# A mixture-of-experts stage on one Trainium2 core: wide and narrow experts of a pair run one after the other, or by turns in slices of 512 gate columns

## The reference, cut to what matters

```
h = rms_norm(x); top 2 of 8 experts by h @ w_router; weights by softmax over the two
for each expert e, for its tokens:
    out += weight * ((silu(h @ w_gate[e]) * (h @ w_up[e])) @ w_down[e])   # 1024 -> 3584 -> 1024
```

## Time and profile before

| what | us |
|---|---|
| median of 3 runs | 1788.53 |
| the profiled execution, and its span | 1787.69, 1785.9 |
| first expert matmul starts | 883.07 |
| first wide expert ends, its narrow one starts | 1002.16 |
| second pair starts | 1107.26 |
| last expert matmul starts | 1776.20 |

### The profile page before, as it was taken

How to read it: one execution, slowest core, us unless ns; L and a number is a source line. 1 busy time by engine, 2 the same in 40 slices (tenths; PEclk the granted TensorE clock), 3 DMA queues, 4 the chain that set the end, 5 groups by cost and what they waited for, 6 DMA issues and landing times.

```text
span 1785.9 us, 22528 instructions
## 1 busy us (share of the span) xinstructions
PE 1677.6 (94%) x8602; PEld 1246.9 (70%) x8602; DVE 1104.5 (62%) x1395; ACT 931.7 (52%) x1162; POOL 21.3 (1%) x30
## 2 busy tenths in 40 slices
PE   9988999999999999999899978999789997899987
PEld 7877788888878888987688524885248852488622
DVE  7985799757668874676898303883029840298400
ACT  6976677556755553664577203773027730277300
POOL 0000000000000000000000000000000000000000
PEclk9999999999999999999999999999999999999988
DMA  9332355544225554334399999999999999999997
GB/s 376 143 112 95 142 189 189 189 171 147 108 95 194 189 197 175 142 142 142 118 370 368 355 422 415 417 372 347 422 415 417 373 344 421 419 418 382 340 422 302
DMA packets 68941, 490.94 MB, mean 275 GB/s; under 512 B 7776, under 2 KB 8160, under 8 KB 9952
## 3 DMA queue, kind: packets, MB, share of 16 engines
q1 hardware_dynamic: 67248, 484.48, 69.5%
q0 software_dynamic: 1584, 4.98, 1.4%
HBM read 485.24 MB, written 4.19 MB: 274 GB/s over the span
## 4 chain that ended last, share of the span: by engine, by line
PE 76%; DMA 12%; DVE 6%; ACT 4%; issue 2%; POOL 0%; SPq 0%; DVEq 0%; ACTq 0%; POOLq 0%
PE ps L460 14%; PE ps L469 13%; PE ps L462 13%; DMA raw<-in_units 12%; PE ps L596 9%; PE ps L1345 8%; PE ps L599 5%; PE ps L480 1%; DVE wl L2360 1%; PE ps L900 1%; PE ps L901 1%; PE ps L905 1%; PE ps L1364 1%; PE ps L1317 1%; PE ps L471 1%
## 5 line engine op out<-in xcount | busy, mean ns | idle before, releaser
L3394 DVE TENSOR_TENSOR wl<-raw,wh 128x2048 fp32r<-128x2048 f32 x160 | 365.6, 2291 | 40.2 <-ACT wh L2238 39.9
L2238 ACT ACTIVATE wh<-raw 128x2048 fp32r<-128x2048 f32 x156 | 299.1, 1917 | 90.0 <-PE ps L469 90.0
L2360 DVE TENSOR_TENSOR wl<-raw,wh 128x2048 fp32r<-128x2048 f32 x124 | 283.0, 2286 | 81.8 <-ACT wh L1564 81.5
L460 PE MATMUL ps<-wh,hT_both 128*128 128x512 f32 (+2 forms) x680 | 268.9, 397 | 15.2 <-ACT wh L2224 8.2
L1564 ACT ACTIVATE wh<-raw 128x2048 fp32r<-128x2048 f32 x125 | 238.4, 1913 | 70.2 <-PE ps L469 69.0
L1345 PE MATMUL ps<-raw,hT_f 128*64 128x512 f32 x448 | 218.7, 637 | 58.5 <-DMA raw<-in_units 58.4
L462 PE MATMUL ps<-wh,hT_both 128*128 128x512 f32 (+2 forms) x680 | 262.5, 388 | 0.0
L3375 DVE TENSOR_TENSOR work<-work,ps 128x256 f32<-128x256 f32 x28 | 11.8, 421 | 370.2 <-ACT work L2212 370.2
L1346 PE MATMUL ps<-raw,hT_f 128*64 128x512 f32 x448 | 219.5, 639 | 0.0
L1345 PEld LDWEIGHTS ps<-raw,hT_f 128*64 128x64 f32 x448 | 61.2, 145 | 188.2 <-issue 188.2
L469 PE MATMUL ps<-wl,hT_both 128*128 128x512 f32 (+2 forms) x680 | 181.9, 385 | 0.2 <-DVE wl L3394 0.2
(11 more groups left out here) (480 smaller groups left out, 2343.8 us busy)
## 6 DMA issues: line engine op xcount, KB each, us to landing
raw<-in_units SPq DMA_DIRECT2D x458, 1024.0 KB, 7.8
x<-in_x SPq DMA_DIRECT2D x2, 512.0 KB, 5.5
work<-in_lru_w SPq DMA_DIRECT2D x1, 1024.0 KB, 15.8
xn<-in_mem SPq DMA_DIRECT2D x1, 1024.0 KB, 15.0
out<-x POOLq DMA_DIRECT2D x2, 512.0 KB, 6.8
consts<-in_consts POOLq DMA_DIRECT2D x1, 768.0 KB, 4.7
consts<-in_consts SPq DMA_DIRECT2D x1, 500.0 KB, 11.8
cols<-in_cols SPq DMA_DIRECT2D x1, 202.0 KB, 2.3
```

Source lines behind the costliest of these rows:

```text
L460: nc.tensor.matmul(out, sh, mh, start=(first and j == 0), stop=False)
L2238: A(wh[:, n % SPLIT, :], raw[:, n % RAW, :], ACT.Copy).then_inc(sem("hi_made"), 1)
L2360: V.tensor_tensor(wl[:, n % SPLIT, :], raw[:, n % RAW, :], wh[:, n % SPLIT, :].bitcast(F32), ALU.subtract).then_inc(sem("lo_made"), 1)
L3394: V.tensor_tensor(wl[:, n % SPLIT, :], raw[:, n % RAW, :], wh[:, n % SPLIT, :].bitcast(F32), ALU.subtract).then_inc(sem("lo_made"), 1)
```

## The change

The two experts of a pair are no longer run one after the other. For each chunk `c` (a slice of 512 gate columns) every engine does the wide expert's part and then the narrow expert's part: TensorE runs wide gate c, up c and down c-1, then narrow gate and up c and down c-1, then the wide chunk's transposes. The order of loads is a table, `STREAM`: per slice 6 wide units (three of them already of the next slice, since splitting runs 3 units ahead) and then 6 narrow ones. At a pair's end the next pair's first three wide units are loaded ahead of the narrow expert's last two. The number of units, matmuls and splits stays the same. The PSUM banks and the small buffers are laid out anew, so that both experts live side by side; both tiny row and weight gathers of a pair move to slice 3, and ScalarE reads both at once. Both address tables are read up front: the queue now waits for `ordered` before it loads the eighth unit of the stage, where before it loaded the whole first wide expert without it.

```diff
+STREAM = [(0, 0, _u) for _u in EXPERT_ORDER[:SPLIT]]
+for _p in range(NPAIR):
+    for _c in range(ECH):
+        _at = 6 * _c + (1 if _c == 0 else -2) + (2 if _c == 0 else 3)
+        _wide = EXPERT_ORDER[_at:_at + (4 if _c == 0 else 6)]
+        STREAM += [(_p, 0, _u) for _u in _wide] + [(_p, 1, _u) for _u in NARROW_ORDER if _u[1] == _c - (_u[0] == "down")]
+    STREAM += [(_p + 1, 0, _u) for _u in EXPERT_ORDER[:SPLIT] if _p + 1 < NPAIR]
+    STREAM += [(_p, 1, ("down", ECH - 1, _h)) for _h in range(2)]
...
@@ TensorE
+            for c in range(ECH):
+                if c > 0:
+                    pe.wait_ge(sem("gate_silu"), ECH * p + c)
+                wide_in("gate", c)
+                if c > 0:
+                    narrow_turned(c - 1)
+                    pe.wait_ge(sem("hidden"), ECH * p + c + 2)
+                wide_in("up", c)
+                if c > 0:
+                    pe.wait_ge(sem("expert_hid"), ECH * p + c)
+                    if c == 1:
+                        pe.wait_ge(sem("y_scaled"), 4 * p + 2)
+                    for half in range(2):
+                        wide_down(c - 1, half)
+                if c == 3:
+                    pe.wait_ge(sem("weighted"), 2 * p + 2)
+                    for i, (places_by, rows_by) in enumerate(((Gw, row_and_gate), (narrow_weights, narrow_rows))):
+                        for t in range(TT):
+                            ins = nc.tensor.matmul(ps[:, 2, 4 * i:4 * i + 4], places_by[:, t, :], rows_by[:, t, :],
+                                                   start=(t == 0), stop=(t == TT - 1))
+                    ins.then_inc(sem("bank7_full"), 2)
...
+                narrow_in(c, 0)
+                if c == ECH - 1:
+                    wide_turned(c)
+                narrow_in(c, 1)
+                if c == ECH - 1:
+                    pe.wait_ge(sem("expert_hid"), ECH * (p + 1))
+                    for half in range(2):
+                        wide_down(c, half)
+                if c > 0:
+                    for half in range(2):
+                        narrow_down(c - 1, half)
+                if c < ECH - 1:
+                    wide_turned(c)
+            narrow_turned(ECH - 1)
+            if not last:
+                pe.wait_ge(sem("chosen"), p + 2)
+                for q in range(4):
+                    gather(q, LATER_BANKS)
+            for half in range(2):
+                narrow_down(ECH - 1, half)
...
@@ SyncE
         def freed(n):
-            s, j = (n - N_FIXED) // E_UNITS, (n - N_FIXED) % E_UNITS
-            if s % 2 == 0:
-                sp_.wait_ge(sem("lo_made"), N_FIXED + s // 2 * E_UNITS + j + 1)
+            p, narrow, what = STREAM[n - N_FIXED]
+            if narrow:
+                sp_.wait_ge(*reached("narrow_gu", p * E_UNITS + NARROW_OF[what] + 1))
             else:
-                sp_.wait_ge(*reached("narrow_gu", s // 2 * E_UNITS + j + 1))
+                sp_.wait_ge(sem("lo_made"), N_FIXED + p * E_UNITS + UNIT_OF[what] + 1)
         sp_.wait_ge(sem("ordered"), 1)
-        for s in range(1, NE):
-            at = nc.sync.value_load(order[0:1, s:s + 1], min_val=N_FIXED, max_val=N_FIXED + (NE - 1) * E_UNITS)
...
+        at = [nc.sync.value_load(order[0:1, s:s + 1], min_val=N_FIXED, max_val=N_FIXED + (NE - 1) * E_UNITS) for s in range(NE)]
+        for n in range(N_FIXED + RAW, N_UNITS):
+            p, narrow, what = STREAM[n - N_FIXED]
+            freed(n - RAW)
+            load(None, n, units_d[at[2 * p + narrow] + UNIT_OF[what]])
@@ ScalarE
+            for c in range(ECH):
+                hi(UNIT_OF["up", c, 1])
+                if c > 0:
+                    hi(UNIT_OF["down", c - 1, 0])
+                    narrow_silu(c - 1)
+                wide_silu(c)
+                if c > 0:
+                    hi(UNIT_OF["down", c - 1, 1])
+                if c == 3:
+                    act.wait_ge(sem("bank7_full"), 6 * p + 6)
+                    act.wait_ge(sem("out_written"), 16 * (TT + 2 * p))
+                    A(both_rows_and_gates, ps[:, 2, 0:8], ACT.Copy).then_inc(sem("bank7_free"), 2)
+                if c < ECH - 1:
+                    for what, half in (("gate", 0), ("gate", 1), ("up", 0)):
+                        hi(UNIT_OF[what, c + 1, half])
+                    narrow_read(c)
+                    hidden_high(c)
...
+            act.wait_ge(sem("unit_used"), E_UNITS * (p + 1) + SPLIT)
+            for h in range(2):
+                A(y[:, h * HALF:(h + 1) * HALF], ps[:, 4 + h, :], ACT.Copy,
+                  scale=slot_row_and_gate[:, 3:4]).then_inc(sem("y_scaled"), 1)
+            narrow_silu(ECH - 1)
+            if not last:
+                for q in range(4):
+                    tokens_high(q, 6 * p + 7 + q, LATER_BANKS)
+                for j in range(SPLIT):
+                    hi(j, p + 1)
+            act.wait_ge(*reached("narrow_gu", E_UNITS * (p + 1)))
+            A(yl, ps[:, 7, :], ACT.Copy, scale=narrow_row_and_gate[:, 3:4]).then_inc(sem("y_scaled"), 2)
@@ VectorE
+            for c in range(ECH):
+                lo(UNIT_OF["up", c, 1])
+                if c > 0:
+                    lo(UNIT_OF["down", c - 1, 0])
+                    narrow_hidden(c - 1)
+                    lo(UNIT_OF["down", c - 1, 1])
+                wide_hidden(c)
+                if c < ECH - 1:
+                    for what, half in (("gate", 0), ("gate", 1), ("up", 0)):
+                        lo(UNIT_OF[what, c + 1, half])
...
+                hidden_low(c)
+                if c == 1:
+                    dve.wait_ge(sem("bank7_full"), 6 * p + 4)
+                    weigh(2 * p, slot)
+                    weigh(2 * p + 1, slot64, narrow_weights, narrow_rows)
+                    if not last:
+                        choose(2 * p + 2)
```

More of the change, by code:

```diff
@@ L1395, in expert, with of, every, bank7 @@
-        def expert(p, i, over=False):
-            of, every, bank7 = counts_of(p, i, over)
+                    expert(p, i)
+        def expert(p, i):
+            def of(m, n):
+                return p * (2 * m) + (NPAIR * m + i * m + n)
+            def every(m, n):
+                return p * (2 * m) + (NE * m + i * m + n)
+            def bank7(k):
+                return p * 6 + (6 * NPAIR + k)
             def rest_of(what):
@@ L1421, in expert @@
                 pe.wait_ge(sem("hidden"), of(ECH, c + 1))
-                if c == 0 and not over and p > 0:
-                    pe.wait_ge(*reached("narrow_first", ECH * p))
                 for u, what in enumerate(("gate", "up")):
@@ L1473, in _ @@
             gather(q)
-        experts()
+        for p in range(NPAIR):
+            pair(p, last=(p == NPAIR - 1))
         pe.wait_ge(sem("routed"), 1)
@@ L2226, in expert, with of, every, bank7 @@
-        def expert(p, i, over=False):
-            of, every, bank7 = counts_of(p, i, over)
+                    expert(p, i)
+        def expert(p, i):
+            def of(m, n):
+                return p * (2 * m) + (NPAIR * m + i * m + n)
+            def every(m, n):
+                return p * (2 * m) + (NE * m + i * m + n)
+            def bank7(k):
+                return p * 6 + (6 * NPAIR + k)
             def hi(j):
-                if not over and j >= E_UNITS:
-                    return
@@ L3349, in over_tables, with weigh @@
             step(V.memset(slots[:, 3 * NE:3 * NE + 2, :], -1.0))
-        def experts():
-            for p in range(NPAIR):
-                expert(p, 0, first=(p == 0))
-                narrow(p, last=(p == NPAIR - 1))
+        def weigh(e, by, weights=Gw, rows_by=row_and_gate):
+            for t in range(TT):
+                V.tensor_scalar(weights[:, t, :], by, places[:, bass.ds(e, 1), t], None, ALU.is_equal)
+            V.tensor_copy(rows_by[:, :, 3], gates[:, bass.ds(e, 1), :]).then_inc(sem("weighted"), 1)
```

304 lines of the change are left out of this document (153 added, 151 removed).

## The result

| | before | after |
|---|---|---|
| median of 4 runs, us | 1788.53 (1787.95 to 1788.64) | 1771.32 (1768.37 to 1773.06) |
| ratio, 95% interval | | 0.9906 [0.9893, 0.9919] |
| profiled execution, and its span | 1787.69, 1785.9 | 1768.37, 1766.5 |
| first, second pair start | 883.07, 1107.26 | 882.26, 1099.98 |

The forecast was 1752 us, its own range 1740 to 1764, the wide one 1730 to 1784: 1771 lies between the two upper ends, and the gain is 17.2 us where 36.5 were forecast. In the changed kernel the numbering is shifted: the wide products are now L465, L467 and L474, the narrow ones L1377 and L1378 (gate, up) and L1394 and L1395 (down), the gather L1322, the splits L2256 and L3457, the load L1555.

A forecast was written before the change was run, and what follows sets the result against it. Loads were to set the pace: 1707.5 us with loads alone, plus 16.2 indirect DMAs, 8.8 holes, 8.5 last TensorE work, 9.6 to the span's end, 1.8 beyond the span: 1752 us; own range 1740 to 1764, wide 1730 to 1784.

The forecast's parts named there:

- slice 3, a pair: ScalarE's wait for tiny matmuls holds up three splits; loads stop 2.2 us once a pair, 8.8 us in all.
- border, beside the loads: Outputs' indirect DMAs cost 4.1 (wide) and 1.3 us (narrow) of loading; nothing added for late splits (bound 3 x 3.1 us).
- start: landing of the 13th load: At the start, the queue is filled from the load issued at 899.9, the 13th of 336, which lands at 904.8 us.
- landing of the last load: At the kernel's end, the last load lands at 1732.5 us, with indirect DMAs (16.2) and slice 3 holes (8.8) counted.
- from there to the end of the span: After the last landing, 8.5 us of TensorE's remaining work, then 9.6 us from the last matmul to the span's end.
- the limit on the rate: Rival: under wide work loads get only 390 GB/s; 36 us more, 1788, no change; chance 0.06.
- the price of a hole: In the load ring, the queue stays filled if a place is free within 12.6 us of its unit's landing.
- the 2.3 us of latency from a lone load: In the load queue, a lone load lands 4.7 us after issue, of which 2.3 us are latency.
- The end: In the last slice, TensorE finishes at T + 38.3 (T: slice's start on TensorE); 9.6 us more to the span's end.
- The clock: Rival: waits in every slice slow TensorE's clock until it becomes the bound; 1763 at 0.92, 1793 at 0.89; chance 0.08.
- small-delays rival: Hand-overs or late splits cost TensorE 1 us more per slice, slack goes, holes count double: 1765 to 1782; chance 0.16.

The follow-up runs named there:

- read after one split: ScalarE reads slice 3's rows and weights behind only the first of the three splits, against the changed kernel; 1759.61 us.
- without indirect DMAs: On top of the late read, plain 64-byte DMAs replace the outputs' indirect DMAs, so experts' results are not added into the output; 1747.38 us.
- late read: ScalarE reads slice 3's rows and weights after the three splits for slice 4, not ahead of them, against the changed kernel; 1755.51 us.
- late read with early splits: On top of the late read, the next pair's first three wide splits go ahead of y, the last narrow chunk and the tokens; 1747.53 us.
- narrow downs first: On top of the late read, the narrow expert's last two down units load ahead of the next pair's first three wide units; 1747.89 us.

## Why the gain was half of the forecast

| term | predicted | after |
|---|---|---|
| slice 3, a pair | 2.2 | 3.9, so 4 x 1.7 = 6.8 more |
| border, beside the loads | 5.4 | 6.8, so 3 x 1.4 = 4.2 more |
| start: landing of the 13th load | 904.8 | 906.2, so 1.4 more |
| rate 421.5, not 422; small gaps | | about 3.3, the rest of the difference |
| landing of the last load | 1732.5 | 1748.2 |
| from there to the end of the span | 18.1 | 18.3 |
| profiled execution | 1752.4 | 1768.4 |
| median above it | 0.8 | 2.9 |

**The mechanism was right.** Loads at 421 GB/s under wide work (the limit on the rate falls), a first pair of 1099.98 - 882.26 = 217.7 us (216 predicted), TensorE's waits in pieces of mostly 1 to 1.5 us (0.3 to 2.35) at narrow units, one hole in slice 3 at the step named, its rest ready at T + 22.25.

**The step that failed** is the price of a hole: "the queue stays filled if each place is free within 6 x 2.485 - 2.3 = 12.6 us of landing", and so "The loads stop for 2.2 us once a pair". Its walk held: the unit landed at T + 7.3 and its place was free at T + 22.25, as predicted, and the load issued into the empty queue needed 4.8 us, so the 2.3 us of latency from a lone load were right. That load is late by the stand less 12.6, to within 0.2 us, in each of ten holes of these runs (stands of 15.1 us four times, 16.3 three times, 18.0 to 19.1 three times). What the step left out is that the queue is not back at its pace with that load: 0.6 to 1.5 us more are lost behind it, and in the read after one split that is nearly the whole loss. As one number for the whole hole, from landing to freeing, the allowance is 10.9 us, and slice 3 costs 14.8 - 10.9 = 3.9, not 2.2.

A likely reason is that the step took the 16 DMA engines to end a load together. In the hole they end apart: the shares above add up to a mean end near 984.3, while the last engine stops near 985.7. A landing is the last engine's, so the others have less queue ahead of them than the landing tells, by some 1.4 us; 2.5 us at the last engine and 1.4 more at the mean one make the 3.9. That the engines end apart is shown; that it is all of the difference is the likeliest reading, not shown apart. The Trainium skill says the same of the landing ("DMA: Bandwidth & Descriptors", section "Why a DMA increments its semaphore by 16 and not by 1"): a DMA's engines finish independently, and only the full count means that all has landed.

**The border** failed by the same step, and by weighing. By the prediction's 15.7 us its units stood for 3 us too long by 12.6 and for 4.8 by 10.9; it was some 16.1 to the freeing, which makes 5.2, and without indirect DMAs 5.7 were lost. I let the larger of two costs stand for both; the larger was the other one.

**The end** came out right by luck. From the last slice's start at 1718.34 TensorE took 39.3 us to the last product's end, with 1.02 us for the last narrow product's operand, where I had 38.3; from there to the end of the span it was 8.8 us, where I had 9.6. The last load landed at T + 29.8, as predicted.

**The clock** played no part in most slices: the granted clock is 1.00 from 990 to 1080, and after waits of 1.15 to 1.30 us products take 0.61 us. It fell at the borders' waits of 4.8 to 5.4 us (0.70 granted from 1110 to 1120), and also in two slices, after waits of 2.19 and 2.13 us (0.57 granted from 1462 to 1466 and from 1677 to 1681); after one of 2.35 us it stayed. The loads do not feel a slow spell: DMA moves 421 GB/s from 1120 to 1200, and from 1681 to 1740. The Trainium skill ("TensorE: Matmul & The Clock Gate", section "HAM oscillation — how this bites in real kernels") tells of a loop whose work in a tile is shorter than its wait for the next load, so that each tile starts at the slow clock. The trace agrees that a long wait brings the slow clock. The prediction had read the section as if each slice were such a tile; with some 28 us of work in a slice against waits of 1 to 2 us it was not.

The small-delays rival (1765 to 1782) holds the measured time, but by another way than its own: TensorE waited for nothing but loads inside the slices, and the late read gave back the holes' full length, so TensorE's slack was not gone and the holes did not count double.

The late read with early splits is the best full version found: 0.9774 [0.9761, 0.9788] of the kernel before, against 0.9906 for the change; 1747.5 us. With the narrow downs first instead it is 0.9783 [0.9770, 0.9797], which these runs do not tell apart.

## What to carry to other kernels

Where a ring of buffers feeds a kernel bound by its loads, follow each unit from landing to the moment when its place is free, and set the longest stand against what the queue ahead of it covers; take the price by a hole that a trace shows, since a lone load's latency tells only how late the first load behind the hole is. An instruction that waits for a late result belongs behind the work that frees places, if nobody needs it sooner, and work put early in an engine's order must have its data by then, or everything behind it pays. A hole and a transfer that fall together are not added, and not read as the one you happened to price: take each away once.

## What the runs showed of the hardware

- The 16 DMA engines of one queue run apart. With the queue running dry, the share fell to nothing over 2.5 us (983.5 to 986), and after a new load was issued at 986.6 it took until 988.5 to be back near full rate.
- A 1 MB load issued into an empty queue landed 4.7 to 4.9 us later. After a hole it was late by its place's stand less 12.6 us, and the loads behind it lost 0.6 to 1.5 us more.
- Plain loads move 420 to 422 GB/s, also while TensorE is busy for all but 6 of 90 us.
- An fp32 matmul with 512 columns shows as two rows with 0.43 us from start to start (L1377: 448 rows for 224 matmuls).
